# Seven block products for eight in part of the value and query projections of a two-layer float32 transformer step

## The reference

```python
kv = _rms_norm(x, kv_norm_g) @ w_kv                    # [256, 2048] @ [2048, 4096]
k = _rms_norm(kv[..., :2048].reshape(b, s, 8, 2, 128), k_norm_g)
v = kv[..., 2048:].reshape(b, s, 8, 256)
h = _rms_norm(x, norm_g)
u = h @ w_in                                           # b_w_in, [2048, 4096]
q = _rms_norm(u[..., :2048].reshape(b, s, 8, 2, 128), q_norm_g) * 128 ** -0.5
z = u[..., 2048:]
# then differential attention of 8 heads on q, k, v, gated by silu(z), and b_w_out
```

## Time and profile before

| what | us |
|---|---|
| median of three runs | 1262.35 |
| the profiled execution, its own time | 1262.53 |
| its span, first to last instruction | 1260.8 |
| TensorE busy / VectorE busy / ScalarE busy in the span | 1251.2 / 792.1 / 766.4 |
| unit 176 (chunk 22) starts at | 504.4 |
| unit 192 (chunk 24) starts at | 547.9 |

### The profile page before, as it was taken

The page is one execution under the profiler, slowest core; times in us unless marked ns, Lnnn a source line. Parts: engine busy times, 40 slices in busy tenths (PEclk is TensorE's granted clock), DMA queues, the critical chain, the costliest instruction groups (busy, mean ns, idle before and its releaser), DMA issues.

```text
span 1260.8 us, 16055 instructions
## 1 busy us (share of the span) xinstructions
PE 1251.2 (99%) x5936; PEld 1044.2 (83%) x5936; DVE 792.1 (63%) x1284; ACT 766.4 (61%) x1208; POOL 204.8 (16%) x149
## 2 busy tenths in 40 slices
PE   9999999999999999999999999999999999999998
PEld 7888888888888888888888888889988888888886
DVE  5497898476657665446677765665544444576545
ACT  5798798765547554445566674446644454666543
POOL 1499999900000000000000010000000000000000
PEclk9999999999999999999999999999999999999999
DMA  9899998954566666666555455567655556655563
GB/s 346 269 256 252 268 254 243 269 164 141 181 195 185 185 186 193 192 195 186 166 155 161 153 167 185 184 191 175 184 165 155 164 154 188 194 167 157 184 193 134
DMA packets 133564, 243.85 MB, mean 193 GB/s; under 512 B 12144, under 2 KB 22512, under 8 KB 133360
## 3 DMA queue, kind: packets, MB, share of 16 engines
q1 hardware_dynamic: 129600, 229.40, 58.7%
q0 software_dynamic: 3600, 13.11, 5.3%
q10 hardware_dynamic: 288, 0.32, 0.1%
HBM read 227.60 MB, written 2.10 MB: 182 GB/s over the span
## 4 chain that ended last, share of the span: by engine, by line
PE 96%; DVE 1%; ACT 1%; DMA 1%; SPq 0%; issue 0%; DVEq 0%; ACTq 0%
PE PS L1579 30%; PE PS L1581 29%; PE PS L1580 29%; PE PS L1504 2%; PE PS L1523 2%; DMA w_raw<-in_a_w_in 1%; PE PS L1707 1%; PE PS L1602 0%; PE PS L1604 0%; PE PS L1603 0%; PE PS L1799 0%; PE PS L1769 0%; PE PS L1781 0%; ACT w_hi L563 0%; DVE stage L1203 0%
## 5 line engine op out<-in xcount | busy, mean ns | idle before, releaser
L1031 DVE TENSOR_TENSOR w_lo<-w_raw,w_hi 128x1024 fp32r<-128x1024 f32 (+1 forms) x339 | 411.3, 1215 | 349.4 <-ACT w_hi L563 348.5
L563 ACT ACTIVATE w_hi<-w_raw 128x1024 fp32r<-128x1024 f32 (+1 forms) x383 | 402.0, 1051 | 364.5 <-PE PS L1581 349.1
L1579 PE MATMUL PS<-w_hi,actB_hi 128*128 128x512 f32 (+1 forms) x752 | 299.0, 398 | 0.0
L1579 PE MATMUL PS<-w_hi,actA_hi 128*128 128x512 f32 x756 | 296.5, 392 | 0.2 <-DVE actA_lo L1046 0.2
L1581 PE MATMUL PS<-w_hi,actA_lo 128*128 128x512 f32 x756 | 295.0, 390 | 0.0
L1580 PE MATMUL PS<-w_lo,actA_hi 128*128 128x512 f32 x756 | 294.7, 390 | 0.0
L1581 PE MATMUL PS<-w_hi,actB_lo 128*128 128x512 f32 (+1 forms) x752 | 291.4, 388 | 0.0
L1580 PE MATMUL PS<-w_lo,actB_hi 128*128 128x512 f32 (+1 forms) x752 | 290.6, 387 | 0.0
L1581 PEld LDWEIGHTS PS<-w_hi,actA_lo 128*128 128x128 f32 x756 | 142.0, 188 | 30.1
L1579 PEld LDWEIGHTS PS<-w_hi,actA_hi 128*128 128x128 f32 x756 | 142.0, 188 | 29.7 <-DVE actA_lo L1046 0.6
L1580 PEld LDWEIGHTS PS<-w_lo,actA_hi 128*128 128x128 f32 x756 | 142.1, 188 | 28.8
(11 more groups left out here) (249 smaller groups left out, 1113.5 us busy)
## 6 DMA issues: line engine op xcount, KB each, us to landing
w_raw<-in_a_w_in SPq DMA_DIRECT2D x95, 512.0 KB, 5.7
w_raw<-in_w_in SPq DMA_DIRECT2D x88, 512.0 KB, 3.7
w_raw<-in_w_kv SPq DMA_DIRECT2D x64, 512.0 KB, 3.8
w_raw<-in_b_w_in SPq DMA_DIRECT2D x64, 512.0 KB, 3.8
w_raw<-in_a_w_out SPq DMA_DIRECT2D x32, 512.0 KB, 3.8
w_raw<-in_b_w_out SPq DMA_DIRECT2D x32, 512.0 KB, 3.7
w_raw<-in_w_out SPq DMA_DIRECT2D x32, 512.0 KB, 4.2
tap_products<-tap_products POOLq DMA_DIRECT2D x25, 512.0 KB, 8.2
```

Of the source, the lines that this page charges most:

```text
L563: nc.scalar.activation(split_slot(u)[0], w_raw[:, RAW_SLOT[u], 0:2 * w], ACT.Copy)\
L1031: V.tensor_tensor(wl, w_raw[:, RAW_SLOT[u], 0:2 * w], wh.bitcast(F32), ALU.subtract)\
L1579: T.matmul(bank, ah, wh[:, kk, :], start=first and kk == 0, stop=False)
```

## The change

Chunks 22 and 23 (the last 1024 value columns) and chunks 24 and 25 (the first 1024 query columns) are computed two at a time. A quad is two k tiles (`kk` 0, 1) by two token halves by two chunks, a product of 2x2 blocks, which takes eight block products, so 24 matmuls in two units. In seven quads this becomes seven products (21 matmuls): unit pairs 176/177, 180/181, 184/185, 188/189 in the values and 196/197, 200/201, 204/205 in the queries. Between them stand plain pairs. The identity needs:

- four sums of activation blocks for each quad (`seven_of_acts`), made ahead for the whole group and split into high and low parts as well. In the values over steps 167 to 172, in the queries over steps 191 to 195;
- four differences of weight blocks for each quad (`differences`, three steps ahead), again split into parts (`differences_lo`); one half of the second unit's own weights isn't needed any more (`HALF_SPLIT`);
- PSUM banks 4 to 7 for four of the seven products, added up on VectorE when a group's quads are done (`join_sevens`, `finish_sevens`).

The values of these chunks are therefore joined in `vals` and scaled there, and the queries in `room_a`, from where they are staged. Query staging of chunks 24 and 25 moves to units 208 to 215.

```diff
+SEVEN = [dict(c=C_V + 2, which="A", quads=(0, 2, 4, 6), kept=0), dict(c=C_Q, which="B", quads=(2, 4, 6), kept=1)]
...
+    UNITS[n:n + 16] = ([(g["c"] + c, i) for c in range(2) for i in range(at)]
+                       + [(g["c"] + c, i) for i in range(at, to) for c in range(2)]
+                       + [(g["c"] + c, i) for c in range(2) for i in range(to, 8)])
...
+KEEP_AT = [FIRST[C_V + 2] - 8, FIRST[C_Q] - 1]
+HALF_SPLIT = {u + 1 for u in SEVEN_AT}
...
+STAGED["q", 0] = [FIRST[C_Q + 2] + at for at in (0, 1, 3)]
+STAGED["q", 1] = [FIRST[C_Q + 2] + at for at in (4, 5, 7)]
...
 ScalarE
+                    if u == g["units"][-1] + 2:
+                        act.wait_ge(S["units_done"], u)
+                        nc.scalar.activation(joined(g["c"], 0), PS[:, 4, :], ACT.Copy).then_inc(S["sevens_first"], 1)
                 for v in splits_at(u):
                     split(v)
+                if u + 2 in SEVEN_AT:
+                    n = SEVEN_AT[u + 2]
+                    for half in range(2):
+                        act.wait_ge(S["sums_made"], 2 * n + half + 1)
+                        nc.scalar.activation(sum_pair_hi(n, half), sum_pair(n, half), ACT.Copy)\
+                            .then_inc(S["sums_hi"], 1)
+                for n, m in enumerate(KEEP_PAIRS):
+                    if u == KEEP_AT[n] + 3:
+                        act.wait_ge(S["sevens_acts"], n + 1)
+                        nc.scalar.activation(seven_acts_hi(m), seven_sums(aux, m), ACT.Copy)\
+                            .then_inc(S["sevens_acts_hi"], 1)
...
 VectorE
+            def differences(u):
...
+                V.tensor_tensor(t1_t3, w_raw[:, at + 1, :].rearrange("p (m n) -> p m n", m=2),
+                                w_raw[:, at:at + 2, 0:NC], ALU.subtract).then_inc(S["sums_made"], 1)
+                dve.wait_ge(S["sums_made"], 2 * n + 1)
+                link(V.tensor_tensor(t2, b22, t1_t3[:, 0, :], ALU.subtract))
+                V.tensor_tensor(t4, b21, t2, ALU.subtract).then_inc(S["sums_made"], 1)
+
+            def differences_lo(u, half):
+                n = SEVEN_AT[u]
+                dve.wait_ge(S["sums_hi"], 2 * n + half + 1)
+                V.tensor_tensor(sum_pair_lo(n, half), sum_pair(n, half),
+                                sum_pair_hi(n, half).bitcast(F32), ALU.subtract).then_inc(S["sums_lo"], 1)
+
+            def seven_of_acts(n, step):
...
+                if step == 0 and n:
+                    V.tensor_tensor(a.rearrange("p k t n -> p k (t n)"), hi[which][:, 0:2 * m, :].bitcast(F32),
+                                    lo[which][:, 0:2 * m, :].bitcast(F32), ALU.add).then_inc(S["sevens_whole"], 1)
+                if step == 1:
+                    dve.wait_ge(S["sevens_whole"], n + 1)
+                    link(V.tensor_tensor(s1, a21, a22, ALU.add))
+                    V.tensor_tensor(s3, a11, a21, ALU.subtract)
+                if step == 2:
+                    link(V.tensor_tensor(s2, s1, a11, ALU.subtract))
+                    V.tensor_tensor(s4, a12, s2, ALU.subtract).then_inc(S["sevens_acts"], 1)
+                if step == 4:
+                    dve.wait_ge(S["sevens_acts_hi"], n + 1)
+                    V.tensor_tensor(seven_sums(aux_r, m), sums_of, seven_acts_hi(m).bitcast(F32), ALU.subtract)\
+                        .then_inc(S["sevens_acts_lo"], 1)
+
+            def join_sevens(n, g, part):
...
+                if part == 0:
+                    dve.wait_ge(S["sevens_first"], n + 1)
+                    link(V.tensor_tensor(c12, PS[:, 5, :], c11, ALU.add))
+                    note(V.tensor_tensor(c21, PS[:, 6, :], c12, ALU.add))
+                else:
+                    dve.wait_ge(S["dve_chain"], n_chain[0])
+                    V.tensor_tensor(c22, PS[:, 7, :], c21, ALU.add)
+                    note(V.tensor_tensor(c12, PS[:, 7, :], c12, ALU.add))
+
+            def finish_sevens(c):
+                chunk_done(dve, c)
+                dve.wait_ge(S["dve_chain"], n_chain[0])
+                for tok in range(TT):
+                    ins = V.tensor_tensor(joined(c, tok), chunk_bank(c, tok), joined(c, tok), ALU.add)
+                ins.then_inc(S["sevens_joined"], 1)
...
 VectorE, in step u
+                if JUST_DONE.get(u) in IN_SEVEN:
+                    finish_sevens(JUST_DONE[u])
                 for v in splits_at(u):
                     split(v)
+                for n in range(2):
+                    seven_of_acts(n, u - KEEP_AT[n])
...
+                if u + 3 in SEVEN_AT:
+                    differences(u + 3)
+                if u + 2 in SEVEN_AT:
+                    differences_lo(u + 2, 0)
+                if u + 1 in SEVEN_AT:
+                    differences_lo(u + 1, 1)
...
 TensorE, seven_products(u)
+                if not second:
...
+                    if opens:
+                        pe.wait_ge(S["t_copied"], COPY_NO["k3"] + 1)
+                        pe.wait_ge(S["sevens_acts_lo"], g["kept"] + 1)
+                    pe.wait_ge(S["lo_ready"], LO_NO[source[c, kts[2 * i + 1]]] + 1)
+                    pe.wait_ge(S[name_lo], n_lo)
+                    one(4, act_parts(0, 0), weight_parts(0), opens, closes)
+                    one(0, act_parts(1, 0), weight_parts(1), i == 0)
+                    if i:
+                        third()
+                    pe.wait_ge(S["sums_lo"], 2 * n + 1)
+                    one(7, act_sums(1), weight_sums(0, 0), opens, closes)
+                    one(6, act_sums(3), weight_sums(0, 1), opens, closes).then_inc(S["units_done"], 1)
+                else:
+                    pe.wait_ge(S["sums_lo"], 2 * n + 2)
+                    one(5, act_sums(2), weight_sums(1, 0), opens, closes)
+                    ins = one(1, act_parts(1, 1), weight_sums(1, 1), i == 0)
```

More of the change, by code:

```diff
@@ L57 @@
 NCH = len(CHUNKS)
+SEVEN = [dict(c=C_V + 2, which="A", quads=(0, 2, 4, 6), kept=0), dict(c=C_Q, which="B", quads=(2, 4, 6), kept=1)]
+for g in SEVEN:
+    plain = [i for i in range(KT // 2) if i not in g["quads"]]
+    order = [0] * KT
+    for n, i in enumerate([*g["quads"], *plain]):
+        order[2 * i:2 * i + 2] = [2 * n, 2 * n + 1]
+    for c in (g["c"], g["c"] + 1):
+        CHUNKS[c] = CHUNKS[c][:3] + (order,) + CHUNKS[c][4:]
+IN_SEVEN = {c: n for n, g in enumerate(SEVEN) for c in (g["c"], g["c"] + 1)}
 UNITS = [(c, i) for c in range(NCH) for i in range(len(CHUNKS[c][3]) // 2)]
@@ L71 @@
 NU = len(UNITS)
+for g in SEVEN:
+    g["units"] = [UNITS.index((g["c"], i)) for i in g["quads"]]
+SEVEN_AT = {u: n for n, u in enumerate(u for g in SEVEN for u in g["units"])}
+BY_PARTS = [n for n, g in enumerate(SEVEN) for _ in g["quads"]]
+KEEP_PAIRS = [max(len(g["quads"]) for g in SEVEN if g["kept"] == n) for n in range(2)]
+KEEP_AT = [FIRST[C_V + 2] - 8, FIRST[C_Q] - 1]
+HALF_SPLIT = {u + 1 for u in SEVEN_AT}
 RAW, RAW_WIDE, PARTS = 4, 6, 3
@@ new lines, in join_sevens @@
+            def join_sevens(n, g, part):
+                c11, c12, c21, c22 = (joined(g["c"] + half, tok) for tok in range(TT) for half in range(2))
+                if part == 0:
[6 more added lines that the diff above has]
+                    note(V.tensor_tensor(c12, PS[:, 7, :], c12, ALU.add))
@@ L1569, in products @@
                 first, last = i == 0, i == len(kts) // 2 - 1
+                opens_last = False
+                if c in IN_SEVEN:
+                    g = SEVEN[IN_SEVEN[c]]
+                    opens_last = c == g["c"] + 1 and i == min(n for n in range(8) if n not in g["quads"])
                 name_lo, n_lo = LO_READY[u]
@@ L1578, in products @@
                         bank = chunk_bank(c, tok)
-                        T.matmul(bank, ah, wh[:, kk, :], start=first and kk == 0, stop=False)
+                        T.matmul(bank, ah, wh[:, kk, :], start=(first or opens_last and tok == 1) and kk == 0, stop=False)
                         T.matmul(bank, ah, wl[:, kk, :], start=False, stop=False)
@@ L1585, in products, with seven_products, act_parts, act_sums @@
                     ins.then_inc(S["tok0_done"], 1)
+            def seven_products(u):
+                c, i = UNITS[u]
+                g = SEVEN[IN_SEVEN[c]]
+                second = c - g["c"]
+                n, q = SEVEN_AT[u - second], g["quads"].index(i)
+                kts, which = CHUNKS[c][3], g["which"]
+                opens, closes = q == 0, q == len(g["quads"]) - 1
+                def act_parts(kk, tok):
+                    k = kts[2 * i + kk]
+                    return [part[which][:, k, tok * P:(tok + 1) * P] for part in (hi, lo)]
+                def act_sums(m):
+                    pairs = KEEP_PAIRS[g["kept"]]
+                    return [part[:, m - 1, q, :] for part in (seven_acts_hi(pairs), seven_sums(aux_r, pairs))]
+                def weight_parts(kk):
+                    return [part[:, kk * NC:(kk + 1) * NC] for part in split_slot(u)]
+                def weight_sums(half, m):
```

(29 more changed lines are left out.)

125 lines of the change are left out of this document (102 added, 23 removed).

## The result

The changed kernel takes 1267.94 us (median of 5 runs, 1267.10 to 1268.45) against 1262.34 for the kernel before: ratio 1.0046, with an interval of 1.0036 to 1.0057. It is 5.6 us slower, although it has 21 matmuls less. The profiled execution took 1268.37 us, with a span of 1266.5.

A forecast was written before the change was run, and what follows sets the result against it. TensorE was taken to bound the kernel. From the profiled 1262.53 us, - 4.76 + 0.92 + 5.48 + 0.92 + 0.2 + 0.1 = 1265.39; with the clock 1267.3; that execution lies 0.18 above the median, so 1267.1; range 1264.0 to 1270.0.

The forecast's parts named there:

- Removed matmuls: In the seven quads on TensorE: 21 matmuls fewer at 0.2266 us each, 4.76 us saved.
- Units 192 and 208: Ends of the value and query groups: each unit waits for VectorE's adds to free its banks, 0.92 us lost each.
- Unit 196: Entry of the query group: first matmul waits for low parts of the activation sums, 5.48 us lost, 0.87 by ScalarE's order.
- The clock: At unit 196: the wait drops the clock to half speed, costing 1.9 us, with ends 0 and 3.7.
- the rival in which it stays up: At unit 196: same waits but no fall of the clock, 1265.2 us; chance 0.22.
- Entry of the value group: Steps 167 to 172: sums and eight ScalarE copies made with queues half free, costed at nothing.
- the rival on loads: Denser quads: loads need 5.2 us, first differences late, ring pushed about 0.55 in four quads, 2.2 more, 1269.3; chance 0.13.
- The transposes of the first query chunk: Behind unit 208: second finish, squares' sums and scaling push this transpose about 0.2 us late.
- the rings that did fit: Inside the groups: longest dependence ring between quads takes 10.22 us against 10.20, rounded up to 0.1 in all.
- the three waits: Waits of TensorE before units 192, 196 and 208: 0.92, 5.48 and 0.92 us, together 7.3.
- Half of the three waits: Rival at units 192, 196 and 208: waits only half as long, 1262.5 us without the clock's part; chance 0.08.

The follow-up runs named there:

- the kernel with the 3.04: Against the kernel with the query group's activation sums on GpSimd: its 128x1536 add there cut into six of 128x256; 1264.28 us, ratio 1.0017.
- the one with the 2.87: Against the changed kernel: ScalarE copies the activation sums first, and GpSimd, not VectorE, makes the query group's whole activations and sums; 1267.00 us, ratio 1.0033.

## Why the prediction was right

The forecast was 1267.1 us, and 1267.94 was measured. The way and the mechanism were right: the wait before unit 196, its place, its length and what ends it, and the fall of the clock. That the number came so close is in part luck, since a term that was missing (the entry of the value group) and two that were too large (the clock and the transposes) nearly cancel. The steps, against the changed kernel's profile:

- *Removed matmuls.* 5915 are there and every undisturbed step is 0.2266 us; -4.76 stands.
- *Units 192 and 208.* 0.92 each was said; 0.98 each was found, put down to L1196. The queue of hand-added steps put the low part of unit 191 at the start of unit 190 and unit 192's banks free 6.36 us later; in the trace that is 541.28 to 547.61, 6.33 us.
- *Unit 196.* 5.48 was said, 5.39 found. Its parts were tested: 0.87 by ScalarE's order (0.89 by experiment), the rest by VectorE's load (a step of 1.67 taken away shortens it by 1.67), and no wait at all once the group opens four units later. The row that bound it is the half part that waited 0.75 for ScalarE with L1177 behind it.
- *The clock.* It fell, as said, and the rival in which it stays up (1265.2) is out for this kernel. The size was taken as 1.9, with ends 0 and 3.7, from a stretch in which nothing ran; no row gave it, so its closeness is luck. The profiled run has 1.4 (0.6 us of the stay at the lower level fell into the wait and cost nothing), and the medians with and without filler differ by 1.9; the stay at 0.50 is 3.4 us in one kernel and 6.8 in another whose pause is shorter. It has no single price.
- *Entry of the value group.* This was costed at nothing, and that was wrong. The differences of unit 180 waited 1.08 us for a load (a load took up to 5.6 us, not 4.8), and TensorE lost 0.49 around units 180 and 181. It lost another 0.17 at the next quad, where VectorE's differences waited for no load, 0.66 in all. The first is the mechanism of the rival on loads, in one place; the two together are a third of its price. The loss is not the same in every execution: some 0.1 us in the profile with two query quads, where the same difference waited 0.65 for its load, and 0.8 in the one with the filled wait; in the query group no step behind the first quad's was more than 0.04 late for its data.
- *The transposes of the first query chunk.* 0.2 was added for them; a wait of 0.23 stood there before the change too. The true term is nothing.
- *The rest.* From the start of unit 176, 504.36 in the trace before, to 648.37, the kernel before takes 144.01 us; the changed one takes 149.11 from 505.04 to 654.15. The terms are -4.76 + 0.98 + 5.39 + 1.40 + 0.98 + 0.66 = 4.65; 0.45 remains, spread over steps of 0.24 where 0.23 is the rule. It was not tested what makes them. The remaining 0.68 us of the profiled execution lie ahead of unit 176, in work that is the same in both. Most of it comes between 31 and 40 us: a load landed late there, ScalarE stood 2.76 us for it, and TensorE had to wait at 34.62. In the other profiles unit 176 starts between 503.64 and 504.56, so this is a difference of executions and not of the change.

For the profiled execution the forecast was 1267.3, and 1268.37 was measured, 1.07 more: +0.66 for the load, +0.45 for the steps, +0.68 ahead of unit 176, -0.5 for the clock, -0.3 for the transposes and for the rings that did fit, and nothing in all for the three waits (+0.12 and -0.09). The waits and the clock that make the kernel slower were all in the sum, with their places; what was missed is about as large as what one execution differs from the next.

Two numbers of the rivals don't follow from the prediction's own terms. Half of the three waits, 3.66 us, taken off 1265.2 is 1261.5 and not 1262.5. And a load of 5.2 us against 5.0 of time makes a quad 0.2 late and not 0.55. Neither enters the forecast.

## What to carry to other kernels

A saved instruction on the bound engine is worth its step only if the engine that prepares for it is not yet full at that place. Count the helper's queue instruction by instruction over the busiest stretch, not its share of the span: 66% busy over the whole was 99% over the ten microseconds that mattered. Where one stretch is full, taking one wait away brings up the next thing that is late (units 192 and 208, then the low parts, then the transposes); leave out the part of the change that stands there (three of 21 matmuls here), and move what is owed to where there is room, until the last consumer is past it. A pause of TensorE can cost more than its length, and filling it with idle matmuls can be faster than waiting (one kernel here, 1.9 us by the medians). Where the clock falls in some executions only, one profile doesn't show what the median is made of: look at the mean clock of every run.

## What the runs showed of the hardware

Which pause brings the granted clock down could not be read from its length alone. In the profiles it fell in pauses of 5.39, 4.50 and 3.72 us and right behind one of 2.87, and it stayed at 1.00 through one of 3.04 us, with dense work at 1.00 before each. By the mean clocks of the single runs, the kernel with the 3.04 seems to see it fall in four or five of its ten executions, and the one with the 2.87 in three of five. The stay at the lower level was 3.4 us in two of the profiles (pauses of 5.39 and 2.87) and 6.8 in another two (4.50 and 3.72).

VectorE and GpSimd hold each other up when both work on operands in SBUF alone: 3.22 us for VectorE's 1.22 beside one add of 4.35, and 1.58 and 1.80 for GpSimd's 0.74 beside VectorE's; VectorE's adds with an operand in PSUM kept their 0.69 beside the long add. Short GpSimd adds only moved the loss: two of VectorE's low parts behind took 1.81 and 1.80.
